# Five unread matmuls ahead of each head's transposes in the latent attention of a two-layer backbone

## The reference

```python
q = ...            # 8 heads, 64 + 32 rotary columns each, from a normed rank 384 projection
k, v = ...         # 8 heads, from a normed rank 256 latent of the context and of the cache
def one_block(qi):                                  # 128 queries
    s = jnp.einsum('bqhd,bkhd->bhqk', qi, k).astype(jnp.float32) * scale
    p = jax.nn.softmax(s, axis=-1).astype(v.dtype)
    return jnp.einsum('bhqk,bkhd->bqhd', p, v)
```

## Time and profile before

| what | value |
|---|---|
| median of 3 runs | 1585.31 us (1584.12 to 1587.62) |
| the profiled execution | 1592.35 us |
| its span, first to last instruction | 1590.6 us |
| TensorE busy | 1306.8 us, 82% of the span |
| VectorE busy | 528.8 us, 33% |
| ScalarE busy | 338.9 us, 21% |
| chain that ended last: TensorE, DMA, VectorE | 59%, 18%, 13% |
| mean granted clock of TensorE | 0.884 |

### The profile page before, as it was taken

One profiled execution on the slowest core, in us unless ns is written; L12 is line 12 of the kernel. 1 busy time (PEld: TensorE's weight loads), 2 busy tenths in 40 slices (PEclk: granted clock), 3 DMA queues, 4 the chain that ended last, 5 costly groups with the idle time before them and its releaser, 6 DMA issues.

```text
span 1590.6 us, 16451 instructions
## 1 busy us (share of the span) xinstructions
PE 1306.8 (82%) x6182; PEld 798.6 (50%) x6182; DVE 528.8 (33%) x1064; ACT 338.9 (21%) x722; POOL 130.4 (8%) x146
## 2 busy tenths in 40 slices
PE   5999799977894998888499997979778859988871
PEld 3545584334694333333256546878767833333321
DVE  3010652322225111010355925677662331110104
ACT  2100313222222111111135314131222301111111
POOL 2400100000002111111000001000000111111100
PEclk9999888777695999899799999989787969999996
DMA  9942565055517799998514200000017259999943
GB/s 343 333 150 106 188 199 212 0 212 212 187 52 286 287 391 418 418 419 353 202 54 150 75 14 0 4 25 1 1 41 264 119 201 407 398 418 418 417 195 122
DMA packets 81300, 329.77 MB, mean 207 GB/s; under 512 B 18791, under 2 KB 19985, under 8 KB 56512
## 3 DMA queue, kind: packets, MB, share of 16 engines
q1 hardware_dynamic: 66224, 300.54, 48.3%
q0 software_dynamic: 14992, 28.10, 5.4%
HBM read 321.09 MB, written 30.58 MB: 221 GB/s over the span
## 4 chain that ended last, share of the span: by engine, by line
PE 59%; DMA 18%; DVE 13%; issue 6%; ACT 2%; SPq 1%; POOL 0%; DVEq 0%; ACTq 0%; POOLq 0%
PE psum L904 20%; PE psum L1218 11%; PE psum L996 9%; DMA ring<-in_moe_w_up 6%; DMA arena<-in_moe_w_up 5%; PE psum L1244 3%; PE psum L928 3%; DMA wide<-in_moe_w_up 3%; PE psum L991 2%; DVE arena L2269 1%; DVE wide L2229 1%; PE psum L1097 1%; PE psum L1117 1%; PE psum L935 1%; DMA arena<-h_rows,slot_token 1%
## 5 line engine op out<-in xcount | busy, mean ns | idle before, releaser
L904 PE MATMUL psum<-wide,ring 128*128 128x384 f32 x704 | 242.9, 506 | 7.0 <-ACT wide L1498 5.1
L904 PEld LDWEIGHTS psum<-wide,ring 128*128 128x128 f32 x704 | 167.4, 240 | 74.7 <-issue 15.4
L1218 PE MATMUL psum<-arena 128*64 128x512 f32 x480 | 160.6, 667 | 24.5 <-DMA ring<-in_moe_w_up 11.8
L1218 PE MATMUL psum<-ring,arena 128*64 128x512 f32 x384 | 133.1, 611 | 12.1 <-DMA wide<-in_moe_w_up 10.8
L996 PE MATMUL psum<-ring 128*128 128x128 f32 x872 | 114.8, 290 | 17.7 <-issue 8.4
L996 PEld LDWEIGHTS psum<-ring 128*128 128x128 f32 x872 | 109.1, 203 | 22.8 <-issue 13.1
L2149 DVE TENSOR_TENSOR arena<-arena,psum 128x256 f32<-128x256 f32 x34 | 14.3, 421 | 315.1 <-ACT arena L1650 315.1
L904 PE MATMUL psum<-ring,wide 128*128 128x512 f32 (+2 forms) x336 | 116.1, 507 | 0.0
L1218 PEld LDWEIGHTS psum<-arena 128*64 128x64 f32 x480 | 49.3, 153 | 108.9 <-issue 105.8
L1218 PE MATMUL psum<-wide,arena 128*64 128x512 f32 x224 | 90.8, 623 | 10.3 <-DMA arena<-in_moe_w_up 10.3
L904 PEld LDWEIGHTS psum<-ring,wide 128*128 128x128 f32 x336 | 58.3, 190 | 57.2 <-issue 56.4
(11 more groups left out here) (483 smaller groups left out, 1683.7 us busy)
## 6 DMA issues: line engine op xcount, KB each, us to landing
ring<-in_ada_w SPq DMA_DIRECT2D x24, 2048.0 KB, 10.7
arena<-in_moe_w_gate SPq DMA_DIRECT2D x28, 1024.0 KB, 15.2
arena<-in_moe_w_up SPq DMA_DIRECT2D x28, 1024.0 KB, 22.6
arena<-in_moe_w_down SPq DMA_DIRECT2D x28, 1024.0 KB, 23.4
ring<-in_moe_w_gate SPq DMA_DIRECT2D x24, 1024.0 KB, 14.6
ring<-in_moe_w_up SPq DMA_DIRECT2D x24, 1024.0 KB, 18.9
ring<-in_moe_w_down SPq DMA_DIRECT2D x24, 1024.0 KB, 20.9
ring<-in_w_in_odd SPq DMA_DIRECT2D x7, 2048.0 KB, 8.1
```

Of the source, the lines that this page charges most:

```text
L904: ins = mm(out, lhs(k), rhs(k), start=(k == 0), stop=(k == n - 1))
L1218: ins = mm(psum[half, 2 + s, :].rearrange("p (w f) -> p w f", w=2), hg[s][:, k, half], buffers[UNITS[q][h] % BUFFERS][0][:, :, k, :], star ...
```

## The change

A helper `keep_busy` issues n matmuls of the identity by the first columns of the constants, which are the identity as well. At each of the 18 heads where no modulation stands, five of them, 128 columns wide, are issued into the bank that the head's transposes will overwrite, ahead of the wait for `probs`. Nothing reads their result. The wait for the bank now sits on the first of them, and the wait for `probs` stays on the transposes. No other engine's stream changes.

```diff
+            def keep_busy(out, n):
+
+                width = out.shape[-1]
+                for _ in range(n):
+                    mm(out, ident, cst[:, 0:width], start=True, stop=True)
+
@@
                     beside("pT", c, h)
                     b = issue("pT", c, h)
+                    if ("pT", c, h) not in parts_at:
+                        keep_busy(b[:, 0:P], 5)
                     pe.wait_ge(S("probs"), n + 1)
                     for t in range(len(tiles)):
                         ins = nc.tensor.transpose(b[:, tok(t)], pr[:, n % 2, tok(t)], ident)
```

## The result

| | kernel before | changed kernel |
|---|---|---|
| median | 1587.13 us (6 runs, 1584.12 to 1590.84) | 1570.97 us (6 runs, 1570.48 to 1577.21) |
| profiled execution | 1592.35 us | 1570.85 us |
| mean clock over the span | 0.884 | 0.907 |

The ratio is 0.9897, with a 95% interval of 0.9880 to 0.9914. The changed kernel's median lies inside the range of 1560 to 1580 and 3.7 us above the 1567.3 that were forecast. Half of these 3.7 us is the kernel before, which measured 1.8 us more here than the 1585.31 from which the forecast started. The saving between the medians is 16.2 us, where 18.0 were forecast.

The account below looks back on a forecast made before the run. TensorE's attention steps at half clock, with waits on VectorE between, were taken as the bound. -17.4 (clock) + 1.4 (head 7) - 2.0 (tail) = -18.0 us, from 1585.31 to 1567.3 us; range 1560 to 1580 us for 8 in 10.

Parts of the forecast that it names:

- The bound and the mechanism: In the attention, TensorE's half-clock steps lengthen the chain; matmuls filling its waits for VectorE raise the clock, giving 17.4 us.
- The fill's price: Each fill takes 1.1 us at full clock and fits in attention holes of 1.33, 1.65 and 1.83 us.
- Heads 7: At head 7 of tiles 0, 1 and 2 no hole covers the fill: 0.5, 0.6 and 0.3 us, together +1.4 us.
- The clock's gift: Attention steps from the `mod_rows` of tile 0, head 1 on run at full clock to its end: 17.4 us saved.
- The sum for the attention: 17.4 us saved by the clock against 1.4 us added at head 7; the attention ends near 406 instead of 422.4 us.
- The tail: Behind the attention, the 36-column matmuls gain at most 3.4 us at full clock; 2 us taken, nothing for the projection behind.
- The arrival at the end: At the kernel's end the whole 18.0 us arrives: no weight load becomes late and the expert weights' stream shifts along.
- The rival in which it is: Expert weight loads behind the attention are bound to something fixed, so the end stays at 1585 us; chance 0.08, shared with gain and overruns in balance.
- the one in which the clock does not follow: The attention's clock stays low despite the fill, nothing is gained and fills overrun: 1593 us; chance 0.12.
- The rival of a partial hold: The clock falls in tile 0, at a `mod` or at head 7; 7 to 9 us less than before, 1577; chance 0.12.
- The rule on idle gaps: Only gaps longer than the attention's holes lower the clock, so the fill changes nothing and the time would be 1593 us.

Follow-up runs that it names:

- cols4: The changed kernel with each fill matmul reading 4 columns of the identity instead of 128; ratio 0.9944 to the kernel before, median 1580.97 us.
- ten: The changed kernel with ten matmuls per fill instead of five; ratio 0.9920 to the kernel before, median 1578.39 us.
- no7: The changed kernel without its fills at head 7 of all three tiles; ratio 0.9896 to the kernel before, median 1573.08 us.
- mod06: The changed kernel with five more unread matmuls directly ahead of the `mod` at tile 0, head 6; ratio 0.9909 to the kernel before, median 1574.69 us.
- second profile of before: The kernel before, unchanged, run and profiled once more; ratio 0.9991 to the kernel before.
- best: The changed kernel with twelve matmuls at (0,0), no fills at (0,7) and (1,7), four more matmuls behind the last products; ratio 0.9860 to the kernel before, median 1568.24 us.
- tiles12: The changed kernel with fills in tiles 1 and 2 alone, none in tile 0; ratio 0.9903 to the kernel before, median 1572.15 us.
- first12: The changed kernel with twelve matmuls instead of five at tile 0, head 0; ratio 0.9874 to the kernel before, median 1571.19 us.

## Why the prediction was right, and where its terms were off

- **The bound and the mechanism.** Confirmed: TensorE's steps are on the chain, the fill lies in VectorE's time, and the gain is the clock's. cols4 takes away the columns and ten the cover, and in the attention they lose 10.6 and 11.0 us of the 17.0.
- **The fill's price.** 0.11 us an instruction, 1.1 a fill, as forecast: 1.12 on the chain. The holes have 0.44 us left, as forecast (0.5); in tile 0 almost nothing, where 0.2 were forecast. The forecast took 1.33 us for tile 0's holes, but only one of the four had that; three had 1.25.
- **Heads 7.** Forecast +0.5 and +0.6 at (0,7) and (1,7). From the end of `mod_rows` to the start of the scores it is now 2.35 us (332.61 to 334.96) and 3.43 us (367.42 to 370.85). Before it was 1.78 us (339.06 to 340.84) and 2.74 us (380.01 to 382.75). So +0.6 and +0.7. At (2,7) 0.3 were forecast and about 0.1 were paid (no7). Together that is the forecast +1.4.
- **The clock's gift, 17.4 us.** Several terms were off and cancelled in part, which is luck. The `mod_rows` of (0,6) was to fall from 6.35 to 3.74 us; it fell to 5.22, since the clock fell at the `mod` ahead of it. That is 1.5 short, and it is the step where I assumed that a clock once up stays up. mod06 points to the cause. The one at (0,1), which I had left as it was, went from 6.44 to 5.39, 1.1 more than forecast. In the second profile of before it took 5.68, so most of that may be chance. The other stretches gave 1.7 us more than summed: 0.3 up to the first `mod_rows`, 0.2 in the rest of tile 0, 0.4 in tile 1 and 0.9 in tile 2.
- **The sum for the attention**, 17.4 - 1.4 = 16.0, against 17.0 measured, or 15.4 against the second profile of before. To the start of the last copy it is 16.8 (422.41 - 305.90 and 403.14 - 303.45).
- **The tail.** 2.0 forecast, 1.6 measured: the 36-column matmuls 5.53 for 7.01, the projection's first part 11.91 for 12.09. That the first could be 3.3 is shown by the 3.73 us of best, ten and tiles12.
- **The arrival at the end.** 18.0 were forecast. In the traces, attention and tail are 18.6 us shorter than in the first profile of before and 17.0 shorter than in the second. From the first scores to the end of the span it is 19.2 and 18.4 us, so nothing of the saving was absorbed behind them. Between the medians it is 16.2, with an interval of about 14 to 19. The rival in which it is, and the one in which the clock does not follow, are out. The rival of a partial hold was true at two places of tile 0 only, in the changed kernel's profile.
- **The rule on idle gaps.** The Trainium skill's rule on the page "TensorE: Matmul & The Clock Gate", section "Why this matters for your kernels", ties a fall of the clock to idle gaps longer than these, and I had set a rival on it. It does not explain the low clock here: the longest idle time of before within tiles 1 and 2 was 1.83 us and the clock was at 0.72 there; filling just these holes brought it to 1.00.

## What to carry to other kernels

Where TensorE's own steps are on the chain and each waits for a short reduction on another engine, look at the granted clock before anything else; a few unread wide matmuls in the wait saved 1% of this kernel's time. Price the fill at full clock against the shortest wait, leave it out where no wait stands, and give it columns: at full clock a fill of 4 columns took 1.01 us and one of 128 took 1.12, but only the wide one brought the clock to 0.97. Three matmuls of 128 columns did here at least what five did, and ten made the attention 11 us longer.

## What the runs showed of the hardware that I had not expected

- As a fill between real matmuls, transposes of float32 held the clock as matmuls do (transposes: 100.60 us at 0.97).
- With the identity as weights, a float32 matmul of 4 columns took about as long as one of 128: 0.10 and 0.11 us for each recorded instruction at full clock (cols4 and the changed kernel).
- With matmuls of 4 columns as the fill the clock was 0.81 at 92% busy, against 0.70 and 0.72 without fill; with one column 0.77. Each is one profile.
- The same instructions run at different clocks from one execution to the next. In the projections ahead of the attention, untouched by any of these edits, 48 recorded matmuls of 512 columns took, before and in the changed kernel:

```profile
281.22 23.83 PE L904 MATMUL psum<-arena 128*64 128x512 f32 x48
```

```profile
281.59 21.01 PE L910 MATMUL psum<-arena 128*64 128x512 f32 x48
```

This is not the change's doing: in the second profile of the kernel before they took 20.96 us. The executions of one kernel differed by 2.7 to 13.7 us from fastest to slowest; how much of that comes from such places is not shown. For changes of 1 or 2 us the length of the changed stretch in the trace says more than the median, but it takes more than one profile, as first12 and best show.
